# The first up-projection of a diffusion backbone as a 2x2 block product with seven products

## What is computed

```python
def conv_ffn(u, w_up, conv_w, conv_b, w_down):
    a, g = jnp.split(u @ w_up, 2, axis=-1)
    a = conv_general_dilated(a, conv_w, ...) + conv_b      # 3 taps along the tokens, each channel alone
    return (jax.nn.gelu(a) * g) @ w_down
# u = rms_norm(h) * (1 + scale) + shift;   h += gate * conv_ffn(u)
# modulations = silu(c) @ mod_w + mod_b: 12 x 1024 values, in two versions (latent and context) where both are used
```

## Time and profile before

| | us |
|---|---|
| runs | 1751.50, 1756.69, 1756.18; median 1756.18 |
| span of the profiled execution | 1756.2 |
| output projection, layer 0, blocks 2 to 7 | 424.8 to 474.8 |
| up-projection, layer 0 | 474.8 to 856.1 |
| down-projection, layer 0 | 856.1 to about 1046 |
| query, key and value blocks | about 1046 to 1227 |

### The profile page before, as it was taken

One profiled execution on the slowest core, in us unless ns is written; L12 is line 12 of the kernel. 1 busy time (PEld: TensorE's weight loads), 2 busy tenths in 40 slices (PEclk: granted clock), 3 DMA queues, 4 the chain that ended last, 5 costly groups with the idle time before them and its releaser, 6 DMA issues.

```text
span 1756.2 us, 26540 instructions
## 1 busy us (share of the span) xinstructions
PE 1706.3 (97%) x9744; PEld 1481.5 (84%) x9744; DVE 931.6 (53%) x1468; ACT 755.4 (43%) x1208; POOL 544.2 (31%) x249
## 2 busy tenths in 40 slices
PE   6999999998999999999999999999999999999997
PEld 2677889897899999999988888987668988888876
DVE  6779977668965666656423364001774522223344
ACT  3573435775433323233333354222884533334442
POOL 1123124453223322223222324222004334444442
PEclk8999999999999999999999999999999999999998
DMA  8323223344334334343221212222322223323221
GB/s 340 140 96 98 96 97 120 122 127 162 120 104 136 132 108 143 109 133 118 87 64 60 70 60 85 72 85 66 103 73 85 73 74 101 99 98 97 93 88 60
DMA packets 66589, 184.08 MB, mean 105 GB/s; under 512 B 5921, under 2 KB 26785, under 8 KB 65201
## 3 DMA queue, kind: packets, MB, share of 16 engines
q1 hardware_dynamic: 44784, 164.69, 27.7%
q10 hardware_dynamic: 21696, 17.88, 3.4%
HBM read 180.40 MB, written 2.15 MB: 104 GB/s over the span
## 4 chain that ended last, share of the span: by engine, by line
PE 84%; DVE 11%; ACT 2%; DMA 1%; issue 1%; POOL 0%; SPq 0%; ACTq 0%; DVEq 0%; POOLq 0%
PE ps L2369 28%; PE ps L2823 13%; PE ps L2368 13%; PE ps L2449 5%; PE ps L2382 4%; PE ps L2820 3%; PE ps L2755 2%; PE ps L2957 2%; PE ps L2936 2%; PE ps L2970 2%; PE ps L2455 1%; DVE raw L1454 1%; PE ps L2352 1%; DVE left L1454 1%; DVE v_a L1495 1%
## 5 line engine op out<-in xcount | busy, mean ns | idle before, releaser
L692 POOL TENSOR_TENSOR wsp<-raw,wsp 128x1024 fp32r<-128x1024 f32 x185 | 457.8, 2475 | 1112.9 <-ACT wsp L762 1112.4
L762 ACT ACTIVATE wsp<-raw 128x1024 fp32r<-128x1024 f32 x185 | 196.3, 1061 | 426.5 <-PE ps L2369 328.1
L2368 PE MATMUL ps<-v_a,wsp 128*128 128x384 f32 x1008 | 342.7, 340 | 0.0
L2369 PE MATMUL ps<-v_b,wsp 128*128 128x386 f32 x1008 | 340.2, 337 | 0.0
L2823 PE MATMUL ps<-hsp,wsp 128*128 128x512 f32 x984 | 277.4, 393 | 2.5 <-DVE hsp L2015 2.5
L2823 PEld LDWEIGHTS ps<-hsp,wsp 128*128 128x128 f32 x984 | 183.6, 188 | 45.6 <-issue 4.4
L2369 PE MATMUL ps<-uf,wsp 128*128 128x512 f32 x888 | 201.4, 389 | 0.0
L2369 PEld LDWEIGHTS ps<-uf,wsp 128*128 128x128 f32 x888 | 166.7, 188 | 34.6
L2369 PEld LDWEIGHTS ps<-v_b,wsp 128*128 128x128 f32 x1008 | 193.5, 192 | 0.0
L2368 PEld LDWEIGHTS ps<-v_a,wsp 128*128 128x128 f32 x1008 | 189.2, 188 | 0.0
L2032 DVE SCALAR_TENSOR_TENSOR conv<-apad,vec,conv 128x770 f32<-128x770 f32 (+1 forms) x44 | 47.7, 1083 | 204.2 <-ACT conv L1199 204.2
(11 more groups left out here) (324 smaller groups left out, 2532.9 us busy)
## 6 DMA issues: line engine op xcount, KB each, us to landing
raw<-in_weights SPq DMA_DIRECT2D x281, 512.0 KB, 3.8
nab<-in_nabias ACTq DMA_DIRECT2D x32, 256.0 KB, 3.0
start_w<-in_start SPq DMA_DIRECT2D x6, 1024.0 KB, 20.9
h<-in_x SPq DMA_DIRECT2D x4, 768.0 KB, 14.3
mD<-rows_scratch ACTq DMA_DIRECT2D x12, 256.0 KB, 4.4
mqs<-rows_scratch ACTq DMA_DIRECT2D x12, 256.0 KB, 5.5
h<-in_x ACTq DMA_DIRECT2D x2, 1536.0 KB, 6.4
start_w<-in_start SPq DMA_DIRECT2D x4, 512.0 KB, 12.4
```

The lines of the kernel that those rows point to most:

```text
L692: pool.tensor_tensor(w[:, 1, :], raw[:, raw_index(s) % 4, :], w[:, 0, :].bitcast(F32), ALU.subtract)\
L762: act.activation(split_of(s)[:, 0, :], raw[:, raw_s % 4, :], ACT.Copy).then_inc(*own.one(hi_ready))
L2368: pe.matmul(cx, w, x_cx[:, k, xp, :], start=first, stop=last)
L2369: mm = pe.matmul(lat, w, x_lat[:, k, xp, :], start=first, stop=last)
```

## The change

**Weights.** With A11, A12 the halves (by K) of a value block's weights and A21, A22 those of the gate block, and with B11, B21 (first half of the tokens) and B12, B22 (second half) the parts of the operand, the four output parts are built from seven products of 4 k-tiles: A11 B11, A12 B21, S1 T1, S2 T2, S3 T3, S4 B22, A22 T4, where S1 = A21 + A22, S2 = S1 - A11, S3 = A11 - A21 and S4 = A12 - S2, up to signs that the host puts into the weights. DVE makes S1, S2 and S4 from the raw tiles into PSUM banks 6 and 7, POOL makes S3; each unit of 128 x 512 is split by ACT (high) and DVE or POOL (low).

**Operand.** T1 to T4 are differences of scaled halves of h, made and split in `combined_high` and `combined_low` in the place of `scaled_high` and `scaled_low`, and `third_operand`.

**Outputs.** Products partly add up in PSUM (three banks a tile, alternating); three are first copied out by ACT (P1, P5, U2), and DVE combines (`c11`, `c12`, `c22`).

**Room.** The new buffers take the place of hidden tiles: 4 stay, 16 are written to DRAM through a ring of two, and come back in two transfers for the down-projection, whose row order changes (`DOWN_ROWS`).

**Modulations.** In the output projection only blocks 0 to 3 still have one; none are left in the up-projection. 18 move into the down-projection, 13 into the query and key blocks, 16 into the value blocks, each with its load in SP's order (`load_order`). The conditioning rows are stored to DRAM and loaded again twice.

```diff
+def load_order():
+
+    order = []
+    for s in range(S_DOWN0):
+        order += [("w", s)] + ([("m", MOD_FIRST + s)] if s < S_MIX else [])
+    order += [("u", n) for n in range(N_UP)]
+    for b in range(FT):
+        order += [("w", S_DOWN0 + b)] + ([("m", M_DOWN + b)] if b < DOWN_MODS else [])
+    for n in range(N_QK):
+        order += [("w", S_QK + n)] + ([("m", M_QK + n - QK_FIRST)] if n >= QK_FIRST else [])
+    for b in range(N_V):
+        order += [("w", S_V1 + b), ("m", M_V + 2 * b), ("m", M_V + 2 * b + 1)]
+    return order + [("w", s) for s in range(S_OUT1, S_END)]
```

SP, in the up-projection's pairs and in the down-projection:

```diff
+                next_load(PLACE["u", 2 * j])
+                next_load(PLACE["u", 2 * j + 1])
+                if H_KEPT <= j - 4:
+                    store_hidden(j - 4)
+            for b in range(FT):
+                r = PLACE["w", S_DOWN0 + b]
+                next_load(r)
+                if b == 2:
+                    sp.wait_ge(*done.at(3, FT - 1))
+                    sp.wait_ge(*done.at(2, FT - 1))
+                    sp.wait_ge(*combined.at("C22", FT - 1))
+                    sp.wait_ge(*done.at(7, FT - 1))
+                    hidden_back(hid0a[:, 0:10, :], 4, 14, back_u)
+                    sp.wait_ge(*done.at(4, FT - 1))
+                    sp.dma_start(c_down[:, :, :], c_d[0].partition_broadcast(P)).then_inc(c_down_loaded.whole.sem, 16)
+                if b < DOWN_MODS:
+                    next_load(r + 1)
+                if b == 0:
+                    store_hidden(18)
+                if b == 1:
+                    store_hidden(19)
+                    for x in range(H_RING):
+                        sp.wait_ge(*hid_stored[x].at(16 * 8))
+                    sp.wait_ge(*done.at(1, FT - 1))
+                    sp.wait_ge(*done.at(5, FT - 1))
+                    hidden_back(hid0b[:, 0:6, :], 14, 20, back_b)
+            for r in range(PLACE["w", S_QK], PLACE["w", S_QK + QK_FIRST] + 1):
+                next_load(r)
+            sp.wait_ge(block_used.sem, S_QK + 1)
+            sp.dma_start(c_late[:, 0, :], c_d[0, 0].partition_broadcast(P)).then_inc(c_late_loaded.whole.sem, 16)
```

ACT, the end of the first operand's high parts, then a pair:

```diff
+                        copy(B21[:, i, 0, cols], h[:, k, toks], act_own, a[:, r:r + 1])
+                    copy(B22[:, i, 0, :], h[:, k, SECOND], q.hi_ready.whole, a[:, 0:1])
+                square(q, k, slice(0, N_TOK), updated)
+                if k < KH:
+                    act.wait_ge(*t_dve.at("T1", i))
+                    copy(T1[:, i, 0, :], tmp[:, i, :], dec_exp)
+                    return
+                if i == 0:
+                    act.wait_ge(*c_stored.at(16))
+                act.wait_ge(*t_dve.at("T2", i))
+                if i == 0:
+                    copy(T2[:, :, 0, SHC], sh_raw[:, 0, :, :], act_own)
+                copy(T2[:, i, 0, 0:HALF], tmp[:, 4 + i % 2, :], dec_exp)
+                act.wait_ge(*t_dve.at("T4", i))
+                copy(T4[:, i, 0, 0:HALF], tmp[:, 6 + i % 2, :], dec_exp)
...
+                def padded(j):
+
+                    par = j % 2
+                    act.wait_ge(q.a_taken.sem, j + 1)
+                    act.wait_ge(*own.last())
+                    if j == 0:
+                        act.wait_ge(*q.pad_zero.at(1))
+                    if j >= 2:
+                        act.wait_ge(q.conv_done.sem, j - 1)
+                    for r, t, a in ((1, CTX, 1), (0, LAT, L0C + 1)):
+                        act.activation(apad0[:, par, a:a + t.stop - t.start], gel0[:, par, t], ACT.Identity,
+                                       bias=bsh[:, par, 0, r:r + 1]).then_inc(*own.one(act_own))
+                    act.wait_ge(*own.last())
+                    c = at_(vec, cv + 4 * j, 0)
+                    act.activation(conv0[:, par, 0:CW], apad0[:, par, 1:1 + CW], ACT.Identity, bias=c(3), scale=c(1))\
+                       .then_inc(*own.one(q.c_ready))
...
+                def pair(j):
+
+                    padded(j - 1)
+                    p1_evicted(j)
+                    if j + 1 < FT:
+                        raw_high("A11", j + 1)
+                    sum_high("S3", j)
+                    p5_evicted(j)
+                    if j + 1 < FT:
+                        sum_high("S1", j + 1)
+                    else:
+                        act.wait_ge(*done.at(5, FT - 1))
+                        high(s_down)
+                    activated(j - 1)
+                    raw_high("A22", j)
+                    u2_evicted(j)
+                    if j + 1 < FT:
+                        sum_high("S2", j + 1)
+                        sum_high("S4", j + 1)
+                        raw_high("A12", j + 1)
+
+                if layer == 0:
+                    first_pair()
+                    for j in range(1, FT):
+                        pair(j)
```

DVE, low parts of the operand, sums, combinations and a pair:

```diff
+                if k < KH:
+                    dve.wait_ge(*t_act.at("B12", i))
+                    for cols, toks, r in FIRST_PARTS:
+                        scaled_less(tmp[:, i, cols], h[:, k, toks], a[:, r:r + 1], tmp[:, 4 + i % 2, cols],
+                                    dve_own if r else row_args)
+                    dve.wait_ge(*q.hi_ready.at(k + 1))
+                    if k == 0:
+                        lower(B11[:, :, 1, SHC], modm[:, 3 * KT:3 * KT + KH, :], B11[:, :, 0, SHC], dve_own)
+                        lower(B21[:, :, 1, SHC], modm[:, 3 * KT + KH:4 * KT, :], B21[:, :, 0, SHC], dve_own)
+                        lower(T4[:, :, 1, SHC], sh_raw[:, 1, :, :], T4[:, :, 0, SHC], dve_own)
+                    for cols, toks, r in FIRST_PARTS:
+                        scaled_less(B11[:, i, 1, cols], h[:, k, toks], a[:, r:r + 1], B11[:, i, 0, cols].bitcast(F32),
+                                    dve_own)
+                    if k:
+                        add_squares(q, k, slice(0, N_TOK))
+                    dve.wait_ge(*t_act.at("T1", i))
+                    dve.wait_ge(*own.last())
+                    lower(T1[:, i, 1, :], tmp[:, i, :], T1[:, i, 0, :], q.lo_ready.whole)
+                    return
...
+            def s1_sum(j):
+
+                r = PLACE["u", 2 * j + 1]
+                dve.wait_ge(raw_loaded[r % 4].sem, 16 * (r // 4 + 1))
+                dve.wait_ge(*own.last())
+                dve.tensor_tensor(ps[:, 6, :], raw_of(2 * j + 1, 0), raw_of(2 * j + 1, 1), ALU.add)\
+                   .then_inc(*own.one(cum_ready))
+
+            def s2_sum(j):
+
+                r = PLACE["u", 2 * j]
+                dve.wait_ge(raw_loaded[r % 4].sem, 16 * (r // 4 + 1))
+                dve.wait_ge(*own.last())
+                dve.tensor_tensor(ps[:, 7, :], ps[:, 6, :], raw_of(2 * j, 0), ALU.add).then_inc(*own.one(cum_ready))
+
+            def s4_sum(j):
+
+                dve.wait_ge(*own.last())
+                dve.tensor_tensor(ps[:, 6, :], ps[:, 7, :], raw_of(2 * j, 1), ALU.add).then_inc(*own.one(cum_ready))
...
+            def c22(j):
+
+                Ba, Bc, Bb = up_banks(j)
+                dve.wait_ge(*done.at(7, j))
+                dve.wait_ge(*own.last())
+                dve.tensor_tensor(ps[:, Bc, 0:HALF], ps[:, Ba, 0:HALF], sP5[:, :], ALU.add).then_inc(*own.one(gsc_ready))
...
+                def g_scaled_out(j):
+
+                    par, (Ba, Bc, Bb) = j % 2, up_banks(j)
+                    dve.wait_ge(*done.at(4, j))
+                    if j >= H_KEPT + H_RING:
+                        dve.wait_ge(*hid_stored[(j - H_KEPT) % H_RING].at(16 * ((j - H_KEPT) // H_RING)))
+                    dve.wait_ge(*own.last())
+                    dve.tensor_scalar(bsh[:, par, 1, :], ps[:, Ba, SHC], -1.0, None, ALU.mult).then_inc(*own.one(dve_own))
+                    dve.scalar_tensor_tensor(out=in_halves(hid_place(j)), in0=ps[:, Ba:Ba + 2, 0:HALF], scalar=-1.0,
+                                             in1=in_halves(rt_row), op0=ALU.mult, op1=ALU.mult)\
+                       .then_inc(*own.one(q.g_taken))
+
+                def hidden(j):
+
+                    par = j % 2
+                    dve.wait_ge(q.gel_ready.sem, j + 1)
+                    dve.wait_ge(*own.last())
+                    for t, r, c0 in ((CTX, 1, 0), (LAT, 0, L0C)):
+                        dve.scalar_tensor_tensor(out=hid_place(j)[:, t], in0=hid_place(j)[:, t],
+                                                 scalar=bsh[:, par, 1, r:r + 1],
+                                                 in1=gel0[:, par, c0:c0 + t.stop - t.start], op0=ALU.add, op1=ALU.mult)\
+                           .then_inc(*own.one(dve_own if r else q.hid_made))
+
+                def pair(j):
+
+                    if j:
+                        c22(j - 1)
+                    if j + 1 < FT:
+                        s1_sum(j + 1)
+                    if j:
+                        conv_taps(j - 1)
+                    if j + 1 < FT:
+                        sum_low("S1", j + 1)
+                        s2_sum(j + 1)
+                    if j:
+                        g_scaled_out(j - 1)
+                        hidden(j - 1)
+                    if j + 1 < FT:
```

(62 more changed lines are left out.)

691 lines of the change are left out of this document (478 added, 213 removed).

## The result

The changed kernel takes 1771.2 us (median of 4 runs, 1768.4 to 1776.0) against 1754.9 (4 runs): ratio 1.0091, 95% interval 1.0068 to 1.0115. It is 16 us slower, where 1751.1 and a range of 1735 to 1774 were given with 0.33 on slower. The profiled execution spans 1769.7, 13.5 more than that of before.

What follows compares the result with a forecast made beforehand. It took PE to bound the kernel before, and DVE's ring of 15.6 us a pair after; 1756.2 - 10.3 (up to down-projection step k = 1) + 5.2 (behind it) = 1751.1 us, range 1735 to 1774.

Steps and rivals of the forecast that it cites:

- the ring: Up-projection, per pair (gate block beside value block): the loop DVE to ACT to DVE takes 14.0 us, 15.6 with the collision.
- the collision: In the ring, POOL takes the port it shares with DVE and delays `hidden`: 1.6 us a pair.
- PE stays the bound: Rival in the pairs: POOL does not hold `hidden`, the ring is under 14.9 us; 14 us less, 1737; chance 0.20.
- Sums in PSUM are dearer: Rival in the ring: four DVE writes to PSUM cost more; at worst ring 16.24, time 1764; chance 0.12.
- Handoffs are dearer: Rival in the ring: some 20 handoffs cost more; at 0.06 us more each, ring 16.8, time 1774; chance 0.18.
- The join: From the output projection into the first pair: h(7) ready at about 490.6, `c22(0)` 40.1 us after 474.8 (bounds 36 and 44).
- the last steps: From the fourth product of pair 20 to the down-projection's step k = 1: 23.1 us together.
- behind the pairs: From the down-projection's step k = 1 on: hidden rows, c and moved modulations cost 5.2 us together.
- c rows: Down-projection: conditioning rows, loaded after the hidden rows, come some 3 us late for DVE at k = 3; 1 us (0 to 5).
- Modulations in the down-projection: Every second step gets a modulation, and a hidden low part can come 0.3 us late: 1 us (0 to 4).
- Query and key blocks: DVE is nearly idle there; three modulations stand before the context's inverse: 0.5 us.
- Start of the attention: The last two modulations stand between the last V copy and the first score bias, and PE waits: 2.7 us.

Runs made afterwards that it cites:

- s3_after_a12: Against the changed kernel, POOL makes the sum S3 for the next tile behind A12's low part, not ahead of it: 1756.8 us.
- c_first: Against the changed kernel, the down-projection's conditioning rows are asked for ahead of the ten hidden rows: 1763.4 us.
- weights_first: Against the changed kernel, each modulation tile of the down-projection lies one weight tile later in SP's order: 1756.7 us.
- qk_weight_first: Against the changed kernel, the first modulation tile of the query and key blocks lies behind the fifth weight tile, not ahead of it: 1764.6 us.
- mods_in_attention: Against the changed kernel, the last two modulations, with bias and scale, move from before the first scores into the attention loop: 1764.5 us.

## Why the prediction failed

**Right: the size of the removal and the ring.** A PE-bound pair takes 14.83 us, as worked out from 0.1766 a matmul. DVE's ring without the collision is 14.35 (14.0 said), the collision 1.03 (1.6 said), together 15.37 (15.6 said); two errors of opposite sign, so the 15.6 was near partly by luck. It sits where it was put, in `hidden`, and PE waits where it was put, for `c22`. The collision was 0.6 too dear because POOL's A22 part was all but over when `hidden` began (563.57 and 563.48), so only S3 held it. Of the rivals, "PE stays the bound" is what s3_after_a12 makes of it. "Sums in PSUM are dearer" is false: 128 x 512 from a PSUM and an SBUF operand into PSUM take 0.70 (L1878) and the low part out of PSUM 0.69 (L1794). The price that the Trainium skill (VectorE: DVE Perf Modes, The TRN2 errata) gives a PSUM source isn't seen in these rows either. "Handoffs are dearer" is false: the gaps in DVE's ring are 0.04 to 0.11.

**Too dear: the join.** h(7) was ready at 483.0, not 490.6, and `c22(0)` came at 509.06 + 0.57, not 514.9. The failing term is the row of DVE's periods in the output projection. From one update of h to the next, m = 1 to 6 took 7.3, 9.9, 9.9, 5.2, 9.5 and 6.4 us, where 10.35 (three times), 7.8, 9.2 and 6.9 were said. I charged POOL's 2.4 us to each step, "for DVE works on SBUF pairs all the time". At m = 4 it doesn't: DVE's update of h reads PSUM there, and POOL's instruction, which began before it, leaves it at its usual length (h's updates start at 449.37 and 454.58, below). At m = 1 DVE's modulation began first, and POOL took 3.3 us. These two steps are 5.6 of the 7.6 us. PE was held by DVE once, for 0.33 us, and block 7 ended at 475.4, not 480.1. The rows below also show what the prediction took from L2058, that an operand in PSUM frees DVE of POOL: of the 22 instructions of that line only one ran beside POOL, and it began first, so they did not show it.

```profile
449.37 0.74 DVE L2417 SCALAR_TENSOR_TENSOR h<-ps,modm,h 128x512 f32<-128x512 f32 x1
...
454.18 0.48 DVE L2414 SCALAR_TENSOR_TENSOR h<-ps,modm,h 128x256 f32<-128x256 f32 x1
454.58 0.74 DVE L2417 SCALAR_TENSOR_TENSOR h<-ps,modm,h 128x512 f32<-128x512 f32 x1
...
454.08 2.41 POOL L796 TENSOR_TENSOR wsp<-raw,wsp 128x1024 fp32r<-128x1024 f32 x1 [7.46 <-ACT wsp L900]
```

The join (5.3 us), 20 rings that took 308.8 us for 312 (3.2; 15.44 each in the mean, a few were longer than 15.37) and the last steps, 21.3 for 23.1 (1.8), make k = 1 come 10.3 us earlier than forecast.

**The step that failed and decided: behind the pairs, 5.2 us.** It was 34.1, and the sign of the change hangs on it. Term by term:
- *c rows, 1 us (0 to 5).* I had them 3 us late; DVE stood 7.5, until they landed at 853.6, and PE 4.4, with matmuls at half clock for some 5 us behind it. The rate was taken rightly (some 400 GB/s there). The next weights came only behind c, for the slot of the first modulation came free at 856, but that tile, 7.2 us late for ACT, held PE no further. c_first: 7.8 us.
- *Modulations in the down-projection, 1 us (0 to 4).* The sentence "asked for some 4 us later than now, with 4 us in hand" failed in places. Where five tiles were 2.1 to 2.3 us late for ACT, PE did not wait. But DVE's modulation beside POOL ends up to 2.2 us later than alone (3.42 for 1.22), and at the turn of the groups it stands behind the updates of h and the squares. SP asked for three tiles only when such a modulation ended (945.7, 957.7 and 999.1), and they were 3.7, 4.8 and 5.8 us late for ACT. The first and the last came out on PE, as 3.4 us at 958.9 (a modulation stood ahead of DVE's low part there as well) and 4.2 at 1008.5. I had priced the case without cover by DVE's 1.8 us, not by a load behind it. weights_first: 14.5 us.
- *Query and key blocks, 0.5.* I looked at DVE, "nearly idle", and did not follow SP past the late c rows, which wait for PE's first query block (36 us) with the fifth weight tile two places behind them. Asked for at 1056.9, that tile came at 1063.9: 5.8 us of PE and 2.6 of slower matmuls. qk_weight_first: 6.6 us.
- *Start of the attention, 2.7.* Right in kind; 3.8 with POOL beside it. mods_in_attention: 4.7 to 6.7 us.

None of the rivals was that one: the side "slower" was there with 0.33, for causes inside the pairs that the trace does not show, and not for the queue, which carries the loss. That 1771.2 lies in the range of 1735 to 1774 is luck: its upper part was drawn for dearer sums and handoffs, and 10.3 us too dear ahead of k = 1 hid a third of the error behind it.

## What to carry to other kernels

When work is moved out of a busy stage, follow the queue that feeds it: every load behind the first is asked for when the moved work frees its slot, so put loads that the bound engine needs ahead of those that only fill a gap, and price a lost cover by the load and the clock behind it, not by the instruction. And where two engines exclude each other, list for each instruction of the one what the other reads at that moment, and which began first; a place in the order can be worth as much as the work itself.
